# Gate and up products of an FFN by seven block products in place of eight, in one block with the output projection

## What is computed

```python
gm = jax.nn.sigmoid(g_mrg)                     # two gates per channel, from a projection of h
y = gm[..., :D_MODEL] * (h_a @ w_a) + gm[..., D_MODEL:] * (o_b @ w_b)
x = x + y @ w_o                                # output projection
gate, up = jnp.split(rmsnorm(x, g_ffn) @ w_ffn_in, 2, axis=-1)
x = x + (jax.nn.silu(gate) * up) @ w_ffn_out
y_prompt, y_sample = rmsnorm(x, g_final)       # split by token
```

## Time and profile before

| | |
|---|---|
| device time, median of 3 runs | 2177.23 us |
| lowest of them | 2171.66 us |
| profiled execution, first to last instruction (span) | 2172.1 us |
| mean granted TensorE clock | 0.962 of full speed |
| TensorE busy, share of the span | 92% |
| VectorE / ScalarE / GpSimd busy | 48% / 35% / 24% |

### The profile page before, as it was taken

How to read it: one execution, slowest core, us unless ns; L and a number is a source line. 1 busy time by engine, 2 the same in 40 slices (tenths; PEclk the granted TensorE clock), 3 DMA queues, 4 the chain that set the end, 5 groups by cost and what they waited for, 6 DMA issues and landing times. The chain is left out here.

```text
span 2172.1 us, 33307 instructions
## 1 busy us (share of the span) xinstructions
PE 2005.7 (92%) x13868; PEld 1860.8 (86%) x13868; DVE 1042.6 (48%) x1753; ACT 770.1 (35%) x1464; POOL 527.8 (24%) x440
## 2 busy tenths in 40 slices
PE   6999999976888868988899999899999999999997
PEld 5999999865666654655899989899999999999997
DVE  6988763466888873323332243533333223322222
ACT  4333333455776751222322223322222234432212
POOL 2545322204654661322011112111111001111000
PEclk8999999986999988999999999999999999999998
DMA  6455531101000016443533332233223333333232
GB/s 207 124 187 164 166 122 39 40 6 40 1 1 20 1 39 224 140 150 112 175 83 93 88 94 64 79 91 94 88 86 97 91 98 101 101 102 93 84 92 63
DMA packets 258148, 203.12 MB, mean 94 GB/s; under 512 B 20342, under 2 KB 237276, under 8 KB 252687
## 3 DMA queue, kind: packets, MB, share of 16 engines
q1 hardware_dynamic: 246399, 150.92, 23.6%
q0 software_dynamic: 6144, 39.46, 5.3%
q10 hardware_dynamic: 5456, 10.62, 1.5%
HBM read 178.59 MB, written 26.54 MB: 94 GB/s over the span
## 5 line engine op out<-in xcount | busy, mean ns | idle before, releaser
L3033 DVE TENSOR_TENSOR ffn_w_l<-ffn_raw,ffn_w_h 128x1024 fp32r<-128x1024 f32 (+1 forms) x136 | 163.9, 1205 | 274.1 <-ACT ffn_w_h L2966 273.8
L98 PE MATMUL banks<-h_h,ffn_w_l 128*128 128x264 f32 x1408 | 287.2, 285 | 5.5 <-DVE ffn_w_l L3033 5.5
L98 PE MATMUL banks<-h_h,ffn_w_h 128*128 128x264 f32 x1408 | 288.2, 286 | 0.0
L98 PE MATMUL banks<-h_l,ffn_w_h 128*128 128x264 f32 x1408 | 287.2, 285 | 0.0
L2966 ACT CAST ffn_w_h<-ffn_raw 128x1024 fp32r<-128x1024 f32 (+1 forms) x136 | 138.6, 1021 | 331.7 <-PE banks L98 330.6
L98 PEld LDWEIGHTS banks<-h_h,ffn_w_l 128*128 128x128 f32 x1408 | 220.4, 189 | 6.0 <-DVE ffn_w_l L3033 5.8
L98 PEld LDWEIGHTS banks<-h_h,ffn_w_h 128*128 128x128 f32 x1408 | 219.4, 189 | 0.0
L98 PEld LDWEIGHTS banks<-h_l,ffn_w_h 128*128 128x128 f32 x1408 | 218.7, 189 | 0.0
L2954 POOL TENSOR_TENSOR act_l_rest<-ffn_act,act_h 128x528 fp32r<-128x528 f32 x38 | 71.7, 1886 | 375.7 <-ACT act_h L2974 375.7
L89 PE MATMUL banks<-fm_hT_h,fm_w_l 128*128 128x352 f32 x648 | 147.7, 336 | 0.8 <-DVE hT_l L918 0.8
L680 POOL TENSOR_TENSOR fm_w_l<-fm_raw,fm_w_h 128x512 fp32r<-128x512 f32 x54 | 93.6, 1734 | 222.0 <-ACT fm_w_h L754 221.9
(11 more groups left out here) (526 smaller groups left out, 4295.1 us busy)
## 6 DMA issues: line engine op xcount, KB each, us to landing
ffn_raw<-in_w_ffn_in_dram SPq DMA_DIRECT2D x88, 512.0 KB, 3.7
ffn_raw<-in_w_ffn_out_dram SPq DMA_DIRECT2D x32, 512.0 KB, 3.9
fm_raw<-in_w_in_dram SPq DMA_DIRECT2D x44, 256.0 KB, 3.0
early_w_raw<-in_w_in_dram SPq DMA_DIRECT2D x32, 256.0 KB, 3.0
merge_raw<-in_w_in_dram SPq DMA_DIRECT2D x32, 256.0 KB, 2.8
ffn_raw<-in_w_ffn_out_dram SPq DMA_DIRECT2D x16, 384.0 KB, 3.4
hT_copy<-fm_hT_h SPq DMA_DIRECT2D x4, 1056.0 KB, 5.2
hT_copy<-hT_l SPq DMA_DIRECT2D x4, 1056.0 KB, 5.3
```

Of the source, the lines that this page charges most:

```text
L98: mm = pe.matmul(out[:, bank, 0:cols.stop - cols.start], w[:, kt, :], x[:, cols], start=(first and n == 0), stop=(last and n == 2))
L3033: dve.tensor_tensor(w_l[n % NSPLIT][:, 0:m, :], raw[n % NRAW][:, 0:m, :], w_h[n % NSPLIT][:, 0:m, :].bitcast(F32), ALU.subtract).then_inc( ...
```

## The change

`stage_merge` and `stage_ffn` become one stage, `stage_back`, with one class `Back` that holds places, lists and semaphores. SBUF is laid out anew so that both fit.

1. **Seven products.** For each feature tile f and token half, gate and up are one 2x2 block product: the weights are (gate, up) x (first, second half of the contraction), the tokens (first, second half of the contraction) x (first, second piece of 264 tokens). Seven products of 4 contraction tiles x 3 matmuls of 264 columns (a "granule", 12 matmuls) take the place of eight such products. Four of the seven use sums of weight blocks, made by GpSimd; the tokens' seven combinations are made by VectorE (`mix_tokens`). The results are put together in two PSUM banks, X and Y, with three copies to SBUF by ScalarE (`keep`) and three additions by VectorE (steps i = 4, 5, 6).
2. **Weights in granules.** Cast and subtraction are made for a granule of 128x512, seven for each f and half, three granules ahead in four slots; the raw weights of an f are 1 MB in two DMAs. The down product takes granules of one contraction tile x 4 output tiles (24 matmuls) and runs in two groups of four output tiles, with the activations split on the fly, twice (`act_high`, `act_lower`).
3. **Output projection per token half**, 2 x 8 feature tiles of 48 matmuls of 264 columns, with its weights loaded twice. The norm's factor of a half is ready before its tokens are mixed: those of the first half are mixed while the second half is projected, those of the second half in the first half's FFN (f = 2, 4, 6, 8), stored to a DRAM buffer and loaded back by GpSimd's queue during the first half's down product.
4. The products with `w_a` and `w_b` use four pieces of 264 columns in place of three of 352. The early rows of the first half are normalised before their transposes.

The core of the diff:

```diff
+    ORDER = ("p1", "p5", "p6", "p3", "p7", "p2", "p4")
+    SUMS = {"p5": 0, "p6": 1, "p3": 2, "p7": 3}
...
+        for hf in range(2):
+            for f in range(FT):
+                loads.append(("in", f, 2))
+                granules += [("in", hf, f, i, len(loads) - 1) for i in range(7)]
+            for grp in range(2):
+                for kt in range(FT):
+                    if kt % 4 == 0:
+                        loads.append(("out", (grp, kt), 1))
+                    granules.append(("out", hf, grp, kt, len(loads) - 1))
...
         @block.gpsimd
+            def sums(hf, f):
+                u, load = FT * hf + f, m.LOADS_HALF * hf + f
+                if u >= 2:
+                    before = m.first_granule(hf, f - 2, 4) if f >= 2 else m.first_granule(0, FT - 2 + f, 4)
+                    pool.wait_ge(m.s_fl, before + 1)
...
+                pool.tensor_tensor(s[:, 0], a21, a22, ALU.add).then_inc(m.s_sum, 1)
+                pool.wait_ge(m.s_sum, 4 * u + 1)
+                pool.tensor_tensor(s[:, 1], s[:, 0], a11, ALU.subtract).then_inc(m.s_sum, 1)
+                pool.wait_ge(m.s_sum, 4 * u + 2)
+                pool.tensor_tensor(s[:, 2], a12, s[:, 1], ALU.subtract).then_inc(m.s_sum, 1)
+                pool.tensor_tensor(s[:, 3], a11, a21, ALU.subtract).then_inc(m.s_sum, 1)
...
+            for hf in range(2):
+                for f in range(FT):
+                    if hf == 0 and f - 1 in MIX_STEPS:
+                        mixed_low(4 + MIX_STEPS.index(f - 1), m.mix_next, m.mix_next_part[0], m.mix_next_part[1])
+                    if hf and f < KD:
+                        add_square(2 * KD + f)
+                    if f + 1 < FT:
+                        sums(hf, f + 1)
...
         @block.scalar
+                if kind == "in":
+                    if i == 1:
+                        keep("p1", u, g - 1)
+                    if i == 2:
+                        keep("p5", u, g - 1)
+                    if i == 3:
+                        keep("u2", u, g - 1)
+                    granule_high(g + AHEAD)
...
+                    if i == 6:
+                        act.wait_ge(m.s_add, 3 * u + 3)
+                        act.activation(rows, rows, ACT.Silu).then_inc(m.s_silu, 1)
+                    if i == 4 and hf and f < KD:
+                        square_tile(2 * KD + f)
...
         @block.vector
+            def mix_tokens(n, mix, hf, kt):
+                rs = m.two(m.half(k.rs, hf))
+                for kd, dst in ((kt, mix[:, 0:4:3, :]), (kt + KB, mix[:, 4:6, :])):
+                    g = k.cols[:, k.c_norm_ffn + kd:k.c_norm_ffn + kd + 1]
+                    ins = dve.scalar_tensor_tensor(dst, m.two(m.half(k.x1[:, kd, :], hf)), g, rs, ALU.mult, ALU.mult)
+                link(ins)
+                link(dve.tensor_tensor(mix[:, 1], mix[:, 3], mix[:, 0], ALU.subtract))
+                link(dve.tensor_tensor(mix[:, 2], mix[:, 5], mix[:, 1], ALU.subtract))
+                dve.tensor_tensor(mix[:, 3], mix[:, 5], mix[:, 3], ALU.subtract)
+                dve.tensor_tensor(mix[:, 6], mix[:, 4], mix[:, 2], ALU.subtract).then_inc(m.s_mix, 1)
...
+                if kind == "in":
+                    if i == 0 and f:
+                        multiply(u - 1, hf, f - 1)
+                    if i == 4:
+                        dve.wait_ge(m.s_fused, g)
+                        dve.tensor_tensor(m.act[hf][:, f, 1], Y, m.kept["u2"][:], ALU.add).then_inc(m.s_add, 1)
+                    if i == 5:
+                        dve.wait_ge(m.s_fused, g)
+                        dve.tensor_tensor(m.kept["p5"][:], X, m.kept["p5"][:], ALU.add).then_inc(m.s_add, 1)
+                    if i == 6:
+                        dve.wait_ge(m.s_fused, g)
+                        dve.tensor_tensor(m.act[hf][:, f, 0], Y, m.kept["p1"][:], ALU.add).then_inc(m.s_add, 1)
+                    granule_low(g + AHEAD)
...
         @block.tensor
+                    bank = Y if name in ("p5", "p3", "p2") else X
...
+                    elif name == "p6":
+                        pe.wait_ge(m.s_keep, 3 * u + 1)
+                    elif name == "p3":
+                        pe.wait_ge(m.s_keep, 3 * u + 2)
+                    elif name == "p7":
+                        pe.wait_ge(m.s_keep, 3 * u + 3)
+                    elif name == "p2":
+                        pe.wait_ge(m.s_add, 3 * u + 1)
+                    else:
+                        pe.wait_ge(m.s_add, 3 * u + 2)
+                    fresh = name in ("p1", "p5", "p2")
+                    for kt in range(KB):
+                        x_h, x_l = m.moving(hf, name, 0, kt), m.moving(hf, name, 1, kt)
+                        for j, (w, x) in enumerate(((w_l, x_h), (w_h, x_l), (w_h, x_h))):
+                            mm = pe.matmul(ps[:, bank, 0:HC], w[:, kt, :], x, start=(fresh and kt == 0 and j == 0),
+                                           stop=(kt == KB - 1 and j == 2), skip_group_check=not fresh)
+                    mm.then_inc(m.s_fused, 1)
```

More of the change, by code:

```diff
@@ L2557, in stage_merge @@
[L2557 to L2566, removed]
@@ L2567, in stage_merge @@
-    HT = TOK // 2
[L2568 to L2591, removed]
@@ new lines, in gate_banks, with banks, pair, half @@
+    def gate_banks(self):
+        return self.k.ps[:, 0:2, 0:self.GH]
+    def banks(self):
+        return self.k.ps[:, 4:8, 0:self.HC]
+    def pair(self, bank):
+        return self.k.ps[:, bank:bank + 2, 0:self.HC]
+    def half(self, t, hf):
+        return t[:, hf * self.HT:(hf + 1) * self.HT]
+    def two(self, t):
+        return t.rearrange("p (c n) -> p c n", c=2)
+    def first_granule(self, hf, f=0, i=0):
+        return self.PER_HALF * hf + 7 * f + i
+    def moving(self, hf, name, part, kt):
+        if hf == 0:
+            return self.mix0[:, self.MIX[name], part, kt, :]
+        return self.mix1[2 * self.ORDER.index(name) + part][:, kt, :]
@@ L2615, in stage_merge, with early_turn, stage_back @@
+    def early_turn(self, hf, f):
+        return f - 13 if hf and 13 <= f < 13 + self.HT // XT else None
+def stage_back(k):
+    nc, ps = k.nc, k.ps
+    m = Back(k)
+    KB, NRAW, NSPLIT, LEAD, NM, NBK = m.KB, m.NRAW, m.NSPLIT, m.LEAD, m.NM, m.NBK
+    HT, HC, GT, AHEAD, NSLOT, FRAW = m.HT, m.HC, m.GT, m.AHEAD, m.NSLOT, m.FRAW
+    NG_ = len(m.granules)
+    NLOAD = len(m.loads)
+    LAST_GATE = NM - 1
+    MIX_STEPS = (2, 4, 6, 8)
     with nc.Block() as block:
@@ L2662, in _ @@
             rows(0)
             rows(1)
[L2664 to L2670 removed]
+            for po in range(2 * KD):
+                rows(po + 2)
+                if po:
+                    add_square(po - 1)
+                if KD + 2 <= po < KD + 6:
+                    kt = po - KD - 2
+                    mixed_low(kt, m.mix, m.mix0[:, :, 0, kt, :], m.mix0[:, :, 1, kt, :])
+                if po == 2 * KD - 2:
+                    sums(0, 0)
@@ new lines, in _, with totals @@
+                        pe.wait_ge(m.s_xl, base + kt0 + kt + 1)
+                    mm = split_product(pe, ps, m.w_h[n % NSPLIT], m.w_l[n % NSPLIT], kt, h, l, kt0 + kt,
+                                       gates if gate else quarters, kt0 + kt == 0, m.ends[n] and kt == KB - 1)
+                mm.then_inc(m.s_used, 1)
+            def totals(n):
+                pe.wait_ge(m.s_ss, 7 * (n + 1))
+                if n:
+                    pe.wait_ge(m.s_ms, n)
+                for c in range(2):
+                    mm = pe.matmul(ps[:, 6 + c, 0:HC], k.ones[:], m.ss[:, c * HC:(c + 1) * HC], start=True, stop=True)
+                mm.then_inc(m.s_tot, 1)
```

1000 lines of the change are left out of this document (558 added, 442 removed).

## The result

The changed kernel takes 2193.6 us (median of 4 runs, 2190.7 to 2197.3), the kernel before 2175.6 beside it: a ratio of 1.0087 with an interval of 1.0067 to 1.0106. That is clear of noise, and by the 2% of this metric still no change. The profiled span is 2192.8 us against 2172.1. The forecast of 2148 is 45 us too low, and the time lies past the top of its range (2190).

The account below looks back on a forecast made before the run. TensorE's matmuls were taken as the bound from 1055 to 2150 us. Removing 72.6 us, less added costs, gave -28.9 against 2172.1: span 2143.2, plus 5.1 for the median, 2148.3; range 2110 to 2190.

Parts of the forecast that it names:

- What is removed: Gate and up fall from 96 to 84 matmuls per unit, 64.7 us; with the stage seam, 72.6 us together.
- the seam: Between the old stages: 5.5 us of TensorE idling and 2.4 us of half-clock matmuls behind it go.
- The lock of the earlier trace: Gate and up: VectorE with two SBUF inputs and GpSimd's reads block each other; 0.33 us per unit, 28 units, +9.2.
- `add_square` ahead of the sums: Second half, f = 0 to 7: GpSimd's sums wait behind the square addition; 1.05 us per unit, +8.4.
- the three things listed: TensorE's expected waits: VectorE's additions in all units, ScalarE's copies in second half's first eight, VectorE's splits after mixing.
- the bounds of 15 and 90: Test of the forecast: wrong if TensorE's listed waits sum to under 15 us or over 90.
- Rival A: Gate and up: sums and splits mesh, TensorE stays the bound; only direct mixing costs remain, 2119 us; chance 0.33.
- Mixing the second half's tokens: First half's FFN, f = 2, 4, 6, 8: 1.35 us late, then about 1.7 in the next unit; +12.2.
- Small ones: Reciprocals of 528 columns on VectorE's list, twice beside granules, and reloads of ScalarE's table; +2 us.
- Mixing the first half's: Projection of the second half, four steps: chain of 7.8 us against 6.7 of TensorE; +7, ends 0 and 15.
- Rival C: Gate and up: short stops let the clock fall, a fifth of 3,696 matmuls at 0.22 us; 2220 us, chance 0.05.
- Rival B: Gate and up: every addition of every unit sits behind a GpSimd sum, 1.7 us per unit; 2206 us, chance 0.12.

Follow-up runs that it names:

- e1: Changed kernel with GpSimd's four weight sums per unit replaced by two constant writes each, so it reads nothing there; 2132.7 us.
- e2: As e1, with GpSimd's sums of squares and low parts of the mixed tokens also replaced by constant writes; 2116.8 us.
- e3: Changed kernel with the next unit's weight sums moved ahead of the low parts and square additions in GpSimd's list; 2193.4 us, ratio 1.0081.
- e8: Changed kernel with all low parts of the mixed tokens made by VectorE, GpSimd keeping the weight sums and squares; 2197.0 us, one run.
- e9: Changed kernel with the two reciprocals of 528 columns inside gate and up replaced by writes of a constant; 2188.5 us, one run.
- e10: As e9, with the eight normalisations of the first half's tokens also replaced by writes of a constant; 2190.2 us, one run.
- e5: Changed kernel with the weight sums (from f = 2 on) and all low parts of the mixed tokens on VectorE, GpSimd keeping the squares; 2146.0 us, ratio 0.9877.

## Why the prediction was wrong

**Right.** What is removed: in e1 a unit that nothing disturbs takes 10.17 us for its 84 matmuls, and nothing stops at the seam. The new groups in one bank cost nothing. The lock of the earlier trace rows as the mechanism; its price in a plain unit (0.33 forecast, about 0.45 measured); `add_square` ahead of the sums (1.05 forecast, 1.34 measured). TensorE's waits name the three things listed, the additions first, then splits and copies, and the splits' mean of 1.18 (raw) and 0.99 (sums) is the "near 1 us against 0.69". DMA hidden. The waits on L3193, L3134 and L2998 sum to 40 us, between the bounds of 15 and 90, and neither half's gate and up has a mean clock under 0.97. Rival A's time is what e2 measured, and its condition, that sums and splits mesh, is what the kernel doesn't meet.

**Wrong: the step "Mixing the second half's tokens", +12.2, "1.35 late" and "about 1.7 late" in the next unit.** It measured 27.9. The first interval is 0.9 over, but the next is 6.1 over. I laid the operations into the list one by one, with their lone durations, and let GpSimd come in with its next four sums as if they were spread over the unit. In fact GpSimd stands still through the mixing and then reads for 14 us with one short pause, and for all of that VectorE's splits take 1.4 to 1.75 us. Even the upper end of 6 per mixing was short of the 7.0. e1 puts 6.1 of the 7.0 on the sums' reading (pair 21.2). That GpSimd's late row of sums is the only way to it is not so: in e3 and e8, where the sums come earlier and fall beside the mixing, a pair costs 28 to 30.

**Wrong: "Small ones", +2.** The first unit measured 4.4 and f = 8 to 12 another 21.6. The step named the reciprocals and forgot that the early normalisations (eight of 528 columns, two SBUF inputs, mean 1.26 us in the changed kernel where 0.76 is the shortest) lie in the same units, behind the end of the square sums with its twelve sums in a row. e9 and e10 give the shares.

**Wrong: "Mixing the first half's", +7.** The projection lost 13.8 us where 3.8 was forecast. I had 7.8 us for a step by a chain with GpSimd's low part at 2.47; it took 3.24 and the step 10.8, as nearly all of VectorE's and GpSimd's work in it reads SBUF with two inputs. Four steps 4.1 over their matmuls are some 16 us, just past the upper end of 15, and e2 confirms the cause (15 us with GpSimd's reads gone).

**Missing altogether: the clock.** Rival C had the half level only as a state of its own. But each of the four stops of 3 us in the mixing pairs is followed by a stretch at 1.2 GHz, 1.5 us in the rows above (not every stop is: after one of 2.7 us at 1881 the matmuls are back at full rate after two), and the clocks of 0.93 in the projection, 0.97 and 0.98 in the FFN's halves bound it: at most 0.07 x 127.6 + 0.03 x 264.6 + 0.02 x 262 = 22 us, part of it fallen in the stops themselves, where it costs nothing. The sum priced the half level for the seam that goes (2.4) and for no stop that comes.

**A reading that was wrong without effect.** The prediction counts two real stops from 1055 us on. There is a third, of 6.8 us, before the first matmul of the merge stage at 1061; the change leaves it nearly as it is (6.1).

**Rival B** was nearer in time (2206) than the forecast, and wrong in its mechanism: not each unit is 1.7 us late, which e1's and the changed kernel's plain units exclude, but ten intervals are 2.6 to 6.1 over. What stays open: counted as use of the one thing, a mixing pair needs 2 x 8.8 + 3.2 + 0.9 + 2.3 = 24.0 us in 20.3, so 3.7 over, near the forecast's 3.05 and not 7.0. About 1.5 of the rest is the clock; the remaining 1.8 is open. One guess is the time in which GpSimd stands and the lock lies idle; e3 and e8, in which it doesn't stand through the mixing, speak against it, as their pairs cost more. The 2.6 us that the first down product took over its forecast were not looked into either.

## What to carry to other kernels

Before handing GpSimd work that reads SBUF, add up for every stretch the two-input SBUF time of VectorE and the reading time of GpSimd as if they were one engine, and look at what stands beside it. Held up, GpSimd makes its reads later in a row (eight and twelve sums here), and VectorE's splits take over twice as long for that time; freed, it makes them beside the next heavy stretch of VectorE (e3, e8). Moving them along the list gained nothing here. As VectorE does the same operation in half the time (0.69 us against 1.28), giving it to VectorE was cheaper than sharing, even at a list that is 86% full (e5). A mean price per unit is not enough: the plain units were forecast well and the loss lay in ten of 42 intervals and in four steps of the projection.

## What the runs showed of the hardware

- A GpSimd operation that only writes doesn't touch VectorE's splits: in e1, 84 splits of raw blocks with a write beside them took 679 to 694 ns; in the changed kernel 98 with a sum, square or low part beside them took 678 to 1841.
- In alternation both are slow: split and sum together take 1.4 to 1.75 us, when alone they take 0.69 and 1.28. GpSimd keeps more of its speed (1.28 to 1.62 or 1.74 us) than VectorE (0.69 to 1.72).
- VectorE's operations with one input in PSUM stay at 0.42 us for 264 columns in the middle of that.
- A stop of TensorE of 2.96 us was followed by about 3.3 us of matmuls at 0.22 us each, starting some 0.9 us after it resumed; a stop of 2.7 us elsewhere was not.
- A reciprocal takes 3.44 us for 528 columns, five times an addition of the same shape (0.70).
